# Down projections of a gated block by seven products of quarters instead of eight, with the operand sums formed on the chip

## The chip, the core and the metric

One core of a Trainium2 chip runs the whole program. The metric is the device time of one execution in microseconds (us), the median of several; less is better. The engines named here are PE (TensorE, matrix products), DVE (VectorE), ACT (ScalarE), POOL (GpSimd) and SP (SyncE, which issues most of the transfers). Each runs its own list of instructions in order, and semaphores order them against each other.

## The reference, cut to what matters

The model has two layers on 1024 tokens of width 1024. The part that is changed is the gated block at the end of each layer, with `D_FF` = 2816:

```python
def conv_glu(h, up, conv, down):
    z = dwconv3(h @ up, conv)
    gate, val = jnp.split(z, 2, -1)
    return (jax.nn.gelu(gate, approximate=True) * val) @ down
```

`h @ up` is (1024 x 1024) by (1024 x 5632), and the last product, called down here, is (1024 x 2816) by (2816 x 1024). In layer 0 the result goes on through `x + gt2 * rmsnorm(y, ...)` into the Fourier mixer of layer 1; in layer 1 it gives the output.

## The kernel before

Every large product is made in three passes on numbers split in two: a matrix is rounded to a high part on ACT (`hi`), the rest is subtracted out on DVE or POOL (`lo`), and PE runs hi by hi, hi by lo and lo by hi (`split_products`, L131 to L133). A matmul instruction takes a 128x128 stationary tile and 512 moving columns.

`conv_glu` runs once for each layer. Its **up** part goes over 22 groups `g` of 128 gate and 128 value channels. The first two are plain; the other 20 (`seven`) form the 2x2 product of quarters with seven products, so a group is 7 x 4 x 3 = 84 matmuls. POOL forms the sums of weight quarters and the low parts (L3138, L3151 to L3162), three products ahead of PE (`RING` = 3); DVE adds the seven results up in PSUM (L3236 to L3255), convolves (L3190, L3193) and multiplies by the gelu (L3199, `product`); SP stores each group's activation to `scr_act` in memory. With PSUM banks `ps1` as `in_m1`, `in_m6`, `in_m7` and `ps0` for value and gate, PE waits for DVE before it writes a bank again.

The **down** part takes the token tiles in three runs, 3, 3 and 2 tiles of 128 tokens (`GROUPS`). In each run it goes over the 22 tiles of `down`'s rows (index `q`, 66 steps in all), with 2 x 3 matmuls for each token tile: 8 x 22 x 6 = 1056. Per step ACT makes the high and DVE the low part of a weight tile (128x1024, unless it is among those kept from the first run) and of an activation tile (128x384). POOL does nothing in down. Operand buffers are a ring of three: ACT may write those of step q only when PE has done step q-3 (`after`). The first two steps' operands are made inside the last up group (`split_part(0)`, `split_part(1)`). The rest of a finished run (square, scale by the row norm, add x, and in layer 0 a second norm, a transposition on PE `turn`, and `features`) is spread over the steps of the next run by rules such as `if k == 3 + 5 * i`; it is class `Tail`, and `follows` is true in layer 0 alone.

## Time and profile before

| what | value |
|---|---|
| median of 3 runs | 2735.75 us (2735.1 to 2738.48) |
| profiled execution, its own span | 2735.4 us |
| PE busy in it | 2545.9 us, 93% of the span |
| DVE, ACT, POOL busy | 57%, 42%, 33% |
| layer 0 `conv_glu`: first and last matmul of down | 1597.25 and about 1855 us |
| layer 1 `conv_glu`: first and last matmul of down | 2485.41 and about 2724.6 us |

The time of the profiled execution and its span are the same to 0.3 us. A PE matmul's row shows 0.39 us, but they overlap: the starts of successive ones are what counts. Times in the rows are us from the start of the span.

### The profile page before, as it was taken

The page shows a single profiled execution, that of the slowest core. Times are in us where ns is not written, and L with a number is a line of the kernel's source. Part 1 is how long each engine was busy: PE and PEld are TensorE (multiplying, and loading weights), DVE is VectorE, ACT ScalarE, POOL GpSimd, SP SyncE. Part 2 cuts the span into 40 slices and gives each one's busy share as a digit, 9 for nine tenths or more (in the row PEclk, how much of TensorE's full clock was granted, in tenths as well). Part 3 has the DMA queues.
Part 4 walks back from the last instruction along what each step waited for, and adds up shares of the span by engine and source line. Part 5 has one row for each costly group of instructions (what it writes and reads, how often), then busy time and mean ns, then how long its engine had stood idle before and what let it go on. Part 6 is the DMA issues. An engine that isn't in the chain of part 4 may idle for free. (4 is left out here: it accounts for less than half of the span.)

```text
span 2735.4 us, 51474 instructions
## 1 busy us (share of the span) xinstructions
PE 2545.9 (93%) x21459; PEld 2056.0 (75%) x21459; DVE 1554.7 (57%) x2258; ACT 1158.6 (42%) x1818; POOL 906.6 (33%) x629
## 2 busy tenths in 40 slices
PE   5998989898999989789999999996988999999998
PEld 4776656566888877678888888775767888888887
DVE  7775622464666646655555564456565555556445
ACT  5211252464555533434444444453443434444434
POOL 2301121212222202247877720001324787772000
PEclk7999999998999989999999999998999999999999
DMA  7686534812222123222323265441222232326554
GB/s 241 216 279 218 174 124 168 255 25 75 77 73 73 50 88 132 77 78 85 93 70 93 82 235 187 167 144 72 85 77 80 82 93 70 92 86 237 188 176 146
DMA packets 295914, 346.27 MB, mean 127 GB/s; under 512 B 28383, under 2 KB 224212, under 8 KB 295684
## 3 DMA queue, kind: packets, MB, share of 16 engines
q1 hardware_dynamic: 286044, 336.64, 37.7%
q10 hardware_dynamic: 9640, 6.33, 0.8%
q8 instruction: 172, 2.82, 0.4%
q14 instruction: 58, 0.48, 0.1%
HBM read 271.58 MB, written 71.34 MB: 125 GB/s over the span
## 5 line engine op out<-in xcount | busy, mean ns | idle before, releaser
L3138 POOL TENSOR_TENSOR cg_u_lo<-cg_u_raw,cg_u_hi 128x512 fp32r<-128x512 f32 x210 | 314.5, 1506 | 148.1 <-ACT cg_u_hi L3024 148.1
L131 PE MATMUL cg_ps<-m_hi,cg_u_hi 128*128 128x512 f32 x844 | 331.5, 393 | 26.1 <-DVE cg_u_lo L3213 21.8
L133 PE MATMUL cg_ps<-m_hi,cg_u_lo 128*128 128x512 f32 x844 | 330.8, 392 | 0.0
L132 PE MATMUL cg_ps<-m_lo,cg_u_hi 128*128 128x512 f32 x808 | 316.3, 391 | 0.0
L3024 ACT ACTIVATE cg_u_hi<-cg_u_raw 128x512 fp32r<-128x512 f32 x216 | 132.1, 629 | 381.0 <-PE cg_ps L133 230.6
L131 PEld LDWEIGHTS cg_ps<-m_hi,cg_u_hi 128*128 128x128 f32 x844 | 160.0, 190 | 61.2 <-DVE cg_u_lo L3213 22.6
L133 PE MATMUL cg_ps<-over_y_tx,cg_u_lo 128*128 128x512 f32 x480 | 186.9, 389 | 0.0
L132 PE MATMUL cg_ps<-over_y_tx,cg_u_hi 128*128 128x512 f32 x480 | 186.9, 389 | 0.0
L131 PE MATMUL cg_ps<-over_y_tx,cg_u_hi 128*128 128x512 f32 x480 | 186.9, 389 | 0.0
L133 PEld LDWEIGHTS cg_ps<-m_hi,cg_u_lo 128*128 128x128 f32 x844 | 159.9, 189 | 33.5
L3190 DVE SCALAR_TENSOR_TENSOR cg_z<-cg_ps,top_conv_f,cg_z 128x1023 f32<-128x1023 f32 x88 | 112.9, 1283 | 115.7 <-ACT cg_z L3048 115.7
L132 PEld LDWEIGHTS cg_ps<-m_lo,cg_u_hi 128*128 128x128 f32 x808 | 152.8, 189 | 31.6
L3138 POOL TENSOR_TENSOR cg_u_lo<-cg_u_s,cg_u_hi 128x512 fp32r<-128x512 f32 x80 | 103.6, 1296 | 63.7 <-ACT cg_u_hi L3024 63.7
L3193 DVE SCALAR_TENSOR_TENSOR cg_z<-cg_ps,top_conv_f,cg_z 128x1023 f32<-128x1023 f32 x88 | 112.9, 1283 | 3.1
L131 PE MATMUL za_ps<-h_hi,za_w_hi 128*128 128x512 f32 x256 | 105.8, 413 | 7.4 <-POOL za_w_lo L1039 7.4
L3048 ACT ACTIVATE cg_z<-cg_ps,top_conv_f 128x1024 f32<-128x1024 f32 x88 | 98.2, 1116 | 21.0 <-DVE cg_ps L3250 11.6
L132 PEld LDWEIGHTS cg_ps<-over_y_tx,cg_u_hi 128*128 128x128 f32 x480 | 90.1, 188 | 18.7
L133 PEld LDWEIGHTS cg_ps<-over_y_tx,cg_u_lo 128*128 128x128 f32 x480 | 90.1, 188 | 18.7
L131 PEld LDWEIGHTS cg_ps<-over_y_tx,cg_u_hi 128*128 128x128 f32 x480 | 90.1, 188 | 18.7
L131 PE MATMUL cg_ps<-over_f_d_hi,cg_a_hi 128*128 128x512 f32 x248 | 97.0, 391 | 6.4 <-DVE cg_a_lo L3209 6.4
L132 PE MATMUL za_ps<-h_lo,za_w_hi 128*128 128x512 f32 x256 | 102.8, 402 | 0.0
L133 PE MATMUL za_ps<-h_hi,za_w_lo 128*128 128x512 f32 x256 | 102.4, 400 | 0.0
(497 smaller groups left out, 6216.2 us busy)
## 6 DMA issues: line engine op xcount, KB each, us to landing
cg_u_raw<-in_ffn_up SPq DMA_DIRECT2D x88, 512.0 KB, 5.1
cg_u_raw<-in_ffn_down SPq DMA_DIRECT2D x64, 512.0 KB, 4.8
qkv_mw<-in_ada_w SPq DMA_DIRECT2D x12, 2048.0 KB
over_f_d_raw<-in_ffn_down SPq DMA_DIRECT2D x48, 512.0 KB, 5.0
scr_act<-cg_z SPq DMA_DIRECT2D x44, 512.0 KB, 2.7
qkv_mw<-in_ada_w SPq DMA_DIRECT2D x8, 1024.0 KB, 11.7
next_w<-in_mix_in SPq DMA_DIRECT2D x16, 512.0 KB, 6.0
za_out<-in_ada_w SPq DMA_DIRECT2D x8, 1024.0 KB
```

Source lines behind the costliest of these rows:

```text
L131: nc.tensor.matmul(out, a_hi, b_hi, start=first, stop=False)
L132: nc.tensor.matmul(out, a_hi, b_lo, start=False, stop=False)
L133: return nc.tensor.matmul(out, a_lo, b_hi, start=False, stop=last)
L3024: A(u_hi[:, n % RING], source(g, i), ACT.Copy).then_inc(uhi_done, 1)
L3048: A(z[:, x, :], both(g, x), ACT.Copy, scale=conv_cols[:, 1, g + x * FT:g + x * FT + 1]).then_inc(mid_done, 1)
L3138: G.tensor_tensor(u_lo[:, n % RING], source(g, i), u_hi[:, n % RING].bitcast(F32), ALU.subtract).then_inc(ulo_done, 1)
L3190: V.scalar_tensor_tensor(z[:, x, 1:S], both(g, x)[:, 0:S - 1], conv_cols[:, 0, c:c + 1], z[:, x, 1:S], ALU.mult, ALU.add).then_inc(left_do ...
L3193: V.scalar_tensor_tensor(z[:, x, 0:S - 1], both(g, x)[:, 1:S], conv_cols[:, 2, c:c + 1], z[:, x, 0:S - 1], ALU.mult, ALU.add).then_inc(con ...
```

## The change

The down product is now a 2x2 product of quarters made with seven products instead of eight, with the same algebra as in up. A (activations) is cut by tokens and by channels, B (down weights) by channels and by output columns; `KD` = 11 tiles of 128 channels are half of the 22, and `HT` = 4 token tiles half of the 8. A step is one (product, k) pair with a 128x512 tile of A and one of B and 4 x 3 = 12 matmuls. There are 77 operand steps (`SPLITS`); the last product (`A22T4`, steps from 66) is run as three passes of 11, over 2, 1 and 1 token tiles, on the same operands. That is 7 x 11 x 4 x 3 = 924 matmuls.

The sums of activations (S1 to S4) are formed on DVE in up, from group 12 on, and once more behind group 21: `activation_sums(g-1)` follows `product(g-1)`. Its partner, the activation of 11 groups earlier, is read back by SP (`load_partner`), and the four sums are stored (`store_sums`, 4 transfers of 256 KB) and read again in down. The sums of weights (T1 to T4) are formed on POOL and (T4) on DVE in down. Weights come from memory once. From step 22 to 65 POOL makes the low parts of B, otherwise DVE does. Results that serve two quarters are copied out by ACT (`keep`) or added by DVE and POOL. Three tail operations move from DVE and ACT to POOL (`add_x`, `scale_x` for token tiles 0 to 3).

```diff
-GROUPS = ((0, 1, 2), (3, 4, 5), (6, 7))
...
+KD = FT // 2
+HT = TT // 2
+A11B11, A12B21, S1T1, S4B22, S2T2, S3T3, A22T4 = range(7)
+STEPS = [(p, k, 0, HT) for p in range(6) for k in range(KD)] + [(A22T4, k, i, n) for i, n in ((0, 2), (2, 1), (3, 1)) for k in range(KD)]
+SPLITS = 7 * KD
+LAST = A22T4 * KD
+TAIL_AT = (59, 61, 63, 65)
+
...
+        def raw_b(n):
+            return (of_b11, of_b21, of_b11, of_b22, of_b22, of_b12, of_b21)[n // KD](n % KD)
...
+            def load_partner(g):
+                if g > KD:
+                    sp.wait_ge(asum_stored, 64 * (g - KD))
+                if g == NG - 1:
+                    sp.wait_ge(umm_done, ITEMS)
+                sp.wait_ge(act_stored, 16 * (g - KD + 1))
+                sp.dma_start(flat(sums_of(g)[:, 0:2, :]), act_d[g - KD]).then_inc(partner_loaded, 16)
+
+            def store_sums(g):
+                sp.wait_ge(asum_done, 4 * (g - KD + 1))
+                for i, at in enumerate((2, 0, 1, 3)):
+                    sp.dma_start(sum_d[i, g - KD], sums_of(g)[:, at, :]).then_inc(asum_stored, 16)
...
+            for n in range(4):
+                load_a(n)
             store_act(NG - 2)
+            store_sums(NG - 2)
             sp.wait_ge(ulo_done, ITEMS)
...
+            load_partner(NG - 1)
+            for k in range(5, KD):
+                sp.dma_start(of_b11(k), down_v[k, 0]).then_inc(b11_loaded[k], 16)
...
+            def split_down_a(n):
+                hi, _ = split_a_to(n)
+                if n >= LAST:
+                    act.wait_ge(a22_loaded[n - LAST], 16)
+                    low_b(act, n)
+                else:
+                    if n == 0:
+                        act.wait_ge(asum_stored, 64 * (SETS - 1))
+                    elif n == 2:
+                        act.wait_ge(umm_done, ITEMS)
+                    elif n >= 3:
+                        after(act, n - 3)
+                    act.wait_ge(a_loaded[n % RAWS], 16 * (n // RAWS + 1))
+                A(hi, raw_a(n), ACT.Copy).then_inc(ahi_done, 1)
...
+            def keep(n):
+
+                for i in range(HT):
+                    if n == A11B11:
+                        product_done(act, n, i)
+                        A(y[:, HT + i, 0:HALF], ps[1][:, i, :], ACT.Copy).then_inc(p1_kept, 1)
...
-                    if g == NG - 1:
-                        split_part(0)
-                        split_part(1)
                     for i in range(2, 5):
                         ahead(n + i + RING)
+                    if g == NG - 1:
+                        for j in range(2):
+                            split_down_a(j)
+                            split_down_b(j)
                     middle(g, VAL)
                     for i in range(5, 7):
                         ahead(n + i + RING)
                     middle(g, GATE)
-            split_part(2)
+            split_down_a(2)
+            split_down_b(2)
             gelu(NG - 1)
...
+            for k in range(KD):
...
+                low_b(pool, k)
+                weight_sum(of_b11(k), of_b12(k), of_b11(k), t1_sum)
+            for k in range(KD):
+                pool.wait_ge(b22_loaded[k], 16)
+                pool.wait_ge(t1_sum, k + 1)
+                weight_sum(of_b12(k), of_b22(k), of_b12(k), t3_sum)
+            for n in range(2 * KD, LAST):
+                p, k = divmod(n, KD)
+                low_weights(n)
+                if p == S4B22:
+                    pool.wait_ge(t3_sum, k + 1)
+                    pool.wait_ge(blo_pool, n - 2 * KD + 1)
+                    weight_sum(of_b22(k), of_b22(k), of_b11(k), t2_sum)
+                if n == S3T3 * KD + 2:
+                    for i in range(HT):
+                        pool.wait_ge(u2_sum, i + 1)
+                        pool.wait_ge(p5_kept, i + 1)
+                        G.tensor_tensor(y[:, HT + i, HALF:D], y[:, HT + i, HALF:D], y[:, HT + i, 0:HALF], ALU.add).then_inc(u4_sum, 1)
+                for t, at in enumerate(TAIL_AT):
+                    if n == at + 1:
+                        tail.add_x(pool, G, t, y[:, t, :])
+                    if n == at + 4 and follows:
+                        scale_x(t)
...
+                z0, z1 = z[:, GATE, 0:HALF], z[:, GATE, HALF:S]
+                p0, p1, s1, s4 = (sums_of(g)[:, i, :] for i in range(4))
+                m = 4 * (g - KD)
+                dve.wait_ge(partner_loaded, 16 * (g - KD + 1))
+                dve.wait_ge(glu_done, g + 1)
+                V.tensor_tensor(s1, p1, z1, ALU.add).then_inc(asum_done, 1)
+                dve.wait_ge(asum_done, m + 1)
+                V.tensor_tensor(p1, p0, p1, ALU.subtract).then_inc(asum_done, 1)
+                dve.wait_ge(asum_done, m + 2)
+                V.tensor_tensor(p0, s1, p0, ALU.subtract).then_inc(asum_done, 1)
+                dve.wait_ge(asum_done, m + 3)
+                V.tensor_tensor(s4, z0, p0, ALU.subtract).then_inc(asum_done, 1)
...
+                    if g > KD:
+                        activation_sums(g - 1)
...
+                    if g == NG - 1:
+                        for j in range(2):
+                            low_down_a(j)
+                            low_down_b(j)
                     convolve(g, GATE)
-            split_part(2)
+            low_down_a(2)
+            low_down_b(2)
             product(NG - 1)
+            activation_sums(NG - 1)
+            for n in range(3, SPLITS):
+                low_down_a(n)
+                if n < 2 * KD:
+                    low_down_b(n)
+                if S2T2 * KD <= n < S2T2 * KD + KD:
+                    last_weight_sum(n - S2T2 * KD)
+                if 46 <= n < 46 + KD:
+                    low_down_b(LAST + n - 46)
...
+                if n == S3T3 * KD + 1:
+                    for i in range(HT):
+                        product_done(dve, S2T2, i)
+                        dve.wait_ge(p1_kept, i + 1)
+                        V.tensor_tensor(y[:, HT + i, 0:HALF], ps[1][:, i, :], y[:, HT + i, 0:HALF], ALU.add).then_inc(u2_sum, 1)
...
+                if n == LAST + 1:
+                    for i in range(HT):
+                        product_done(dve, S3T3, i)
+                        dve.wait_ge(u4_sum, i + 1)
+                        V.tensor_tensor(y[:, HT + i, HALF:D], ps[1][:, i, :], y[:, HT + i, HALF:D], ALU.add).then_inc(y22_done, 1)
+                for t, at in enumerate(TAIL_AT):
+                    if n == at + 1:
+                        residual(t)
...
+            def down(n):
+                p, k, first_tile, count = STEPS[n]
+                at = n if n < SPLITS else LAST + k
+                more = p in (A12B21, S4B22, A22T4)
+                side_of = ps[0] if p in (S1T1, S4B22) else ps[1]
+                (a_hi, a_lo), (b_hi, b_lo) = split_a_to(at), split_b_to(at)
+                pe.wait_ge(alo_done, at + 1)
+                low_b(pe, at)
+                for i in range(first_tile, first_tile + count):
+                    tile = slice(i * P, (i + 1) * P)
+                    if k == 0:
+                        if p == A11B11:
                             pe.wait_ge(u3_done, NG - PLAIN)
+                        elif p == A12B21:
+                            pe.wait_ge(p1_kept, i + 1)
+                        elif p == S1T1:
+                            pe.wait_ge(conv_done, 2 * NG)
+                        elif p == S4B22:
+                            pe.wait_ge(p5_kept, i + 1)
+                        elif p == S2T2:
+                            pe.wait_ge(y11_done, i + 1)
+                        elif p == S3T3:
+                            pe.wait_ge(u2_sum, i + 1)
+                        else:
+                            pe.wait_ge(y22_done, i + 1)
```

Two places in the order of instructions. First **DVE in the last up group (g = 21) of layer 0** and behind it. `cg0_z` is the activation, `cg0_u2`, `cg0_u3`, `cg0_m1` hold partial results; a `_lo` tile is a low part. Before:

```order
L3199 TENSOR_TENSOR cg0_z<-cg0_z 128x1024
L3207 TENSOR_TENSOR over_f_d_lo<-over_f_d_raw,over_f_d_hi 128x1024
L3209 TENSOR_TENSOR cg0_a_lo<-cg0_a_raw,cg0_a_hi 128x384
L3207 TENSOR_TENSOR over_f_d_lo<-over_f_d_raw,over_f_d_hi 128x1024
L3209 TENSOR_TENSOR cg0_a_lo<-cg0_a_raw,cg0_a_hi 128x384
L3245 TENSOR_TENSOR cg0_u2<-cg0_ps0,cg0_u2 128x512
L3248 TENSOR_TENSOR cg0_ps0<-cg0_ps0,cg0_u3 128x512
L3250 TENSOR_TENSOR cg0_ps0<-cg0_ps0,cg0_u3 128x512
L3190 SCALAR_TENSOR_TENSOR cg0_z<-cg0_ps0,top_conv_f,cg0_z 128x1023
L3193 SCALAR_TENSOR_TENSOR cg0_z<-cg0_ps0,top_conv_f,cg0_z 128x1023
L3253 TENSOR_TENSOR cg0_ps0<-cg0_ps0,cg0_m1 128x512
L3255 TENSOR_TENSOR cg0_ps0<-cg0_ps0,cg0_u2 128x512
```

Of the change, from the last sum of group 20 to the operands of steps 0 and 1:

```order
L3398 TENSOR_TENSOR cg0_over_ring_sums<-cg0_z,cg0_over_ring_sums 128x512
L3455 TENSOR_TENSOR cg0_u2<-cg0_ps0,cg0_u2 128x512
L3458 TENSOR_TENSOR cg0_ps0<-cg0_ps0,cg0_u3 128x512
L3460 TENSOR_TENSOR cg0_ps0<-cg0_ps0,cg0_u3 128x512
L3374 SCALAR_TENSOR_TENSOR cg0_z<-cg0_ps0,top_conv_f,cg0_z 128x1023
L3377 SCALAR_TENSOR_TENSOR cg0_z<-cg0_ps0,top_conv_f,cg0_z 128x1023
L3463 TENSOR_TENSOR cg0_ps0<-cg0_ps0,cg0_m1 128x512
L3465 TENSOR_TENSOR cg0_ps0<-cg0_ps0,cg0_u2 128x512
L3403 TENSOR_TENSOR cg0_a_lo<-cg0_u_raw,cg0_a_hi 128x512
L3408 TENSOR_TENSOR cg0_b_lo<-raw_over_f_b,cg0_b_hi 128x512
L3403 TENSOR_TENSOR cg0_a_lo<-cg0_u_raw,cg0_a_hi 128x512
L3408 TENSOR_TENSOR cg0_b_lo<-raw_over_f_b,cg0_b_hi 128x512
```

The four operations that make operands for steps 0 and 1 stood ahead of the two convolutions and wait for ACT alone; now they stand behind `L3465`, the last addition of the group. A little further on DVE comes to the operands of steps 2 and 3, with the product and the sums of group 21 between them (`y0_x` holds that last set):

```order
L3403 TENSOR_TENSOR cg0_u_lo<-cg0_u_raw,cg0_u_hi 128x512
L3408 TENSOR_TENSOR cg0_u_lo<-raw_over_f_b,cg0_u_hi 128x512
L3383 TENSOR_TENSOR cg0_z<-cg0_z 128x1024
L3392 TENSOR_TENSOR y0_x<-y0_x,cg0_z 128x512
L3394 TENSOR_TENSOR y0_x<-y0_x 128x512
L3396 TENSOR_TENSOR y0_x<-y0_x 128x512
L3398 TENSOR_TENSOR y0_x<-cg0_z,y0_x 128x512
L3403 TENSOR_TENSOR cg0_a_lo<-cg0_u_raw,cg0_a_hi 128x512
L3408 TENSOR_TENSOR cg0_b_lo<-raw_over_f_b,cg0_b_hi 128x512
```

Step 2's operands stand ahead of `L3383`, step 3's behind the four sums. Now **ACT at the same place**, before:

```order
L3052 ACTIVATE cg0_z<-cg0_z 128x1024
L3062 ACTIVATE over_f_d_hi<-over_f_d_raw 128x1024
L3065 ACTIVATE cg0_a_hi<-cg0_a_raw 128x384
L3062 ACTIVATE over_f_d_hi<-over_f_d_raw 128x1024
L3065 ACTIVATE cg0_a_hi<-cg0_a_raw 128x384
L3024 ACTIVATE cg0_u_hi<-cg0_u_raw 128x512
L3024 ACTIVATE cg0_u_hi<-cg0_u_s 128x512
L3048 ACTIVATE cg0_z<-cg0_ps0,top_conv_f 128x1024 x2
```

and of the change:

```order
L3135 ACTIVATE cg0_z<-cg0_z 128x1024
L3107 ACTIVATE cg0_u_hi<-cg0_u_raw 128x512
L3107 ACTIVATE cg0_u_hi<-cg0_u_s 128x512
L3150 ACTIVATE cg0_a_hi<-cg0_u_raw 128x512
L3173 ACTIVATE cg0_b_hi<-raw_over_f_b 128x512
L3150 ACTIVATE cg0_a_hi<-cg0_u_raw 128x512
L3173 ACTIVATE cg0_b_hi<-raw_over_f_b 128x512
L3131 ACTIVATE cg0_z<-cg0_ps0,top_conv_f 128x1024 x2
```

The two middle copies (`cg0_z<-cg0_ps0`) followed the up splits; now four splits of down stand ahead of them, the first of which waits until the sums of group 20 are stored. Last, **POOL in steps 56 to 63** of down, where before it had no instruction (`L3315` is a low part of B, `L3338` the additions to `y`, `L2341` add_x, `L3278` scale_x):

```order
L3315 TENSOR_TENSOR cg_u_lo<-raw_over_f_b,cg_u_hi 128x512
L3315 TENSOR_TENSOR cg_b_lo<-raw_over_f_b,cg_b_hi 128x512
L3338 TENSOR_TENSOR y_y<-y_y 128x512 x4
L3315 TENSOR_TENSOR cg_b_lo<-raw_over_f_b,cg_b_hi 128x512
L3315 TENSOR_TENSOR cg_u_lo<-raw_over_f_b,cg_u_hi 128x512
L3315 TENSOR_TENSOR cg_b_lo<-raw_over_f_b,cg_b_hi 128x512
L2341 TENSOR_TENSOR y_x<-y_x,y_y 128x1024
L3315 TENSOR_TENSOR cg_b_lo<-raw_over_f_b,cg_b_hi 128x512
L3315 TENSOR_TENSOR cg_u_lo<-raw_over_f_b,cg_u_hi 128x512
L2341 TENSOR_TENSOR y_x<-y_x,y_y 128x1024
```

## Rows read from the trace of the kernel before

**Rows 1.** The page, part 1: busy us, share of the span, instructions.

```profile
PE 2545.9 (93%) x21459; PEld 2056.0 (75%) x21459; DVE 1554.7 (57%) x2258; ACT 1158.6 (42%) x1818; POOL 906.6 (33%) x629
```

**Rows 2.** Windows: one up group, down's middle, a tail; busy us, clock, DMA, GB/s.

```profile
1457.00:1476.04 19.04, 19.04 (x86) 15.77 (x85) 11.05 (x13) 7.98 (x11) 15.02 (x12) 1.00 0.27 83
...
1597.00:1620.00 23.00, 22.31 (x99) 18.14 (x98) 15.67 (x18) 10.37 (x14) 0.00 (x0) 1.00 0.81 299
...
2600.00:2724.60 124.60, 124.60 (x551) 103.22 (x550) 61.25 (x79) 51.30 (x80) 0.00 (x0) 1.00 0.50 164
```

**Rows 3.** Timeline, PE: first matmuls of down in both layers, and one turn.

```profile
1597.25 0.39 PE L131 MATMUL cg_ps<-over_f_d_hi,cg_a_hi 128*128 128x512 f32 x1
...
1825.50 1.03 PE L2352 MATMUL cg_ps<-top_ident,y_y 128*128 128x128 f32 x8
...
2485.41 0.39 PE L131 MATMUL cg_ps<-over_f_d_hi,cg_a_hi 128*128 128x512 f32 x1
```

**Rows 4.** Timeline, ACT: squares of the last token tile of each layer.

```profile
1855.22 1.02 ACT L2261 ACTIVATE over_h_rows<-cg_ps 128x1024 f32<-128x1024 f32 x1
...
2725.94 1.02 ACT L2261 ACTIVATE over_h_rows<-cg_ps 128x1024 f32<-128x1024 f32 x1
```

**Rows 5.** Timeline, DVE, one steady group of up; in brackets idle before.

```profile
1464.17 0.70 DVE L3255 TENSOR_TENSOR cg_ps<-cg_ps,cg_u 128x512 f32<-128x512 f32 x1 [0.34 <-PE cg_ps L133]
...
1467.37 1.28 DVE L3193 SCALAR_TENSOR_TENSOR cg_z<-cg_ps,top_conv_f,cg_z 128x1023 f32<-128x1023 f32 x1
...
1472.94 1.22 DVE L3199 TENSOR_TENSOR cg_z<-cg_z 128x1024 f32<-128x1024 f32 x1
```

**Rows 6.** Timeline, POOL, in the same group.

```profile
1458.30 1.29 POOL L3151 TENSOR_TENSOR cg_u_s<-cg_u_raw 128x512 f32<-128x512 f32 x1 [0.17 <-POOL cg_u_lo L3138]
...
1462.35 1.30 POOL L3157 TENSOR_TENSOR cg_u_raw<-cg_u_s,cg_u_raw 128x512 f32<-128x512 f32 x1
1464.53 2.55 POOL L3138 TENSOR_TENSOR cg_u_lo<-cg_u_raw,cg_u_hi 128x512 fp32r<-128x512 f32 x2 [0.89 <-ACT cg_u_hi L3024]
...
1473.10 2.20 POOL L3138 TENSOR_TENSOR cg_u_lo<-cg_u_raw,cg_u_hi 128x512 fp32r<-128x512 f32 x1 [0.16 <-ACT cg_u_hi L3024]
```

**Rows 7.** Timeline, DVE and POOL in layer 0's last up group.

```profile
1589.45 1.65 DVE L3209 TENSOR_TENSOR cg_a_lo<-cg_a_raw,cg_a_hi 128x384 fp32r<-128x384 f32 x1
...
1593.26 0.55 DVE L3209 TENSOR_TENSOR cg_a_lo<-cg_a_raw,cg_a_hi 128x384 fp32r<-128x384 f32 x1
...
1588.82 1.87 POOL L3138 TENSOR_TENSOR cg_u_lo<-cg_u_raw,cg_u_hi 128x512 fp32r<-128x512 f32 x1 [1.64 <-ACT cg_u_hi L3024]
1590.64 1.61 POOL L3138 TENSOR_TENSOR cg_u_lo<-cg_u_s,cg_u_hi 128x512 fp32r<-128x512 f32 x1
```

**Rows 8.** One line's ns min/median/max; then groups: total us, mean ns | idle.

```profile
L3213 DVE TENSOR_TENSOR cg_u_lo<-cg_u_raw,cg_u_hi x6: 683/692/693, 1169.7 to 2060.8; 128x512 fp32r<-128x512 f32 x6
...
L2309 DVE SCALAR_TENSOR_TENSOR y_y<-y_y,cg_t_rstd,over_h_rows 128x1024 f32<-128x1024 f32 x12 | 15.4, 1286 | 0.4
...
L3024 ACT ACTIVATE cg_u_hi<-cg_u_s 128x512 fp32r<-128x512 f32 x80 | 50.4, 629 | 80.1 <-PE cg_ps L133 78.9 <-issue 1.2
...
L3545 POOL TENSOR_TENSOR m_lo<-fft_over_f_f,m_hi 128x1024 fp32r<-128x1024 f32 x8 | 18.9, 2363 | 45.9 <-ACT m_hi L3510 45.9
```

**Rows 9.** Timeline, PE, after 10.26 us and after 2.93 us of idleness.

```profile
1170.42 0.80 PE L131 MATMUL cg_ps<-m_hi,cg_u_hi 128*128 128x512 f32 x1 [10.26 <-DVE cg_u_lo L3213]
...
1175.63 0.40 PE L131 MATMUL cg_ps<-m_hi,cg_u_hi 128*128 128x512 f32 x1
...
1812.88 0.47 PE L131 MATMUL cg_ps<-m_hi,cg_u_hi 128*128 128x512 f32 x1 [2.93 <-DVE cg_u_lo L3209]
...
1817.30 0.39 PE L131 MATMUL cg_ps<-over_f_d_hi,cg_a_hi 128*128 128x512 f32 x1
```

**Rows 10.** Issue of a store on SP (ns min/median/max); transfers, KB, us to landing.

```profile
L2958 SPq DMA_DIRECT2D scr_act<-cg_z x44: 320/339/339, 1208.8 to 2495.4; - x44
...
scr_act<-cg_z SPq DMA_DIRECT2D x44, 512.0 KB, 2.7
...
cg_u_raw<-in_ffn_down SPq DMA_DIRECT2D x64, 512.0 KB, 4.8
```

476 lines of the change are left out of this document (294 added, 182 removed).

## The prediction

> **What bounds the kernel now.** The page's first lines say that PE is the engine that counts: 93% of the span, with DVE at 57%, ACT at 42% and POOL at 33% [rows 1]. The windows by stage say how it differs inside `conv_glu` [rows 2]: in a steady up group PE is busy for all of 19.04 us at full clock, beside DVE 11.05 and POOL 15.02; in down PE is full again while POOL has nothing. Down of layer 1 runs from 2485.41 [rows 3] to the last tile's square at 2725.94 [rows 4], the matmuls ending about 2724.7: 1056 matmuls in 239.4 us, 0.2267 us each (a group of 84 is 19.04). Down of layer 0 runs from 1597.25 to about 1855.1, 257.9 us: 239.4 of matmuls, six turns inside at up to 1.0 us [rows 3], and 12.5 us of waits, one of 2.93 [rows 9]. So fewer matmuls shorten the span only while ACT, DVE and POOL deliver operands within the new, shorter steps.
>
> Two things of this trace decide how well they can. First, **DVE and POOL block each other** when DVE reads two SBUF operands [rows 7]: a 384-wide subtraction takes 0.55 us alone, but 1.65 when POOL has got in first; POOL's, begun at 1588.82, ends at 1590.69, the DVE one 0.41 later, and POOL's next, begun at 1590.64, shows 1.61 instead of 1.29: it ends at 1592.25, 1.15 after DVE's 1591.10. They alternate. For 512 columns DVE takes 0.69 alone [rows 8] and, once it has waited, 0.14 less, 0.55; POOL takes 1.29 alone [rows 6] and 1.15 once it has waited. Additions with one operand in PSUM show no such wait (0.70 with POOL busy) [rows 5, 6]. Second, **a pause of PE costs more than itself** [rows 9]: after 10.26 us idle the next twelve matmuls take 5.21 us (1170.42 to 1175.63) where 2.72 is usual, so 2.5 more at the 1.2 GHz level; after 2.93 idle, 4.42, so 1.7 more.
>
> **What is won.** 132 matmuls a layer less, 264 x 0.2267 = 59.9 us. Layer 0's 12.5 us of waits belong to rules that are gone; I count them as won and cost the new waits below. At the end one token tile is left instead of two: in layer 1 what follows the last matmul is one addition (0.70), a square (1.5), reciprocal and scale (1.4) and add (1.2) beside two scales and adds in series, 1.5 us less; in layer 0 I estimate 2.5 less. Together 76.4 us.
>
> **Start of down (S).** Times from the last up group's start, taken from the steady group, which begins at 1464.0 (PE ended just ahead of the addition at 1464.17) [rows 5]. The product of group 20, at 8.9 there (1472.94), comes at about 10.6 to 11.8, since the sums of the group before push DVE (below). Four sums, chained, with POOL's last low part between: 15.8. SP issues four stores at 0.34 each, the last lands 2.7 after its issue [rows 10]: 19.9. Only then does ACT split steps 0 and 1 (4 x 0.56 back to back, 0.63 alone [rows 8]): 22.2, then the value copy 1.12: 23.4. DVE: two convolutions 2.6, two additions 1.3, 27.4; a and b of step 0 1.3: 28.7. PE finished up at 19.1: **9.6 us idle**. In before these splits stood ahead and PE went on without a gap [rows 3]. Then steps 0 to 2 run to 37.7 (0.8 lost on step 2, whose low parts stand behind a convolution). Step 3's stand behind product 21 (ends 36.1), a 512 KB store, the partner's load (lands near 41; 2.7 to 4.8 after its issue [rows 10]) and four sums (44.1): ready at 45.4. PE waits **7.8** more. S = 18.2 a layer, 36.4; bounds 13 and 22 (sums without blocking and landing in 2.7; 4.8 twice). The two pauses a layer bring 4 x 2.5 = 10 us of low clock.
>
> **Up groups with sums (U),** ten a layer. POOL's run from `L3151` to the next group's second low part ends at 1465.8, PE needs it at 1466.7: 0.9 us to spare [rows 6]. The sums fall on that run; each waits one POOL operation and pushes one: the four take 5.9 us, POOL is late by two or three times 0.55. PE loses about 0.6 a group, 12 us in all. Low end 0. High end: if DVE becomes the bound with 11.05 of work, 2.4 waiting for the two middle copies [rows 5] and 4 x (0.69 + 1.29) for the sums, 21.4 us a group, 2.3 more than 19.04: 46.
>
> **Steps 22 to 54 (CD).** A step is 12 x 0.2267 = 2.72 us. In S1T1 the port has DVE 0.69 and POOL 1.29, which fits. In S4B22 POOL has two: 0.55 + 1.15 + 1.29 + 0.1 for its own semaphore = 3.1. With three buffers POOL begins 2.65 us early, which is used up in seven of eleven steps; 1.5 us lost. In S2T2 DVE has three and POOL one: 0.69 + 1.15 + 0.55 + 0.61 = 3.0, and nothing is to spare: 3.1 lost. 4.6 a layer, and 0.7 at step 22, whose POOL operation stands behind the last T3 sum: 10.6 in all. Bounds: 0, were the lead never used up, and 20, were each operation at 0.69 + 1.29. Of this port the Trainium skill says the same as the rows (SBUF — State Buffer, Who interferes with whom: a DVE instruction with two SBUF inputs and a POOL one that reads SBUF exclude each other for the whole instruction). It goes further than they do for `scale_y`, which reads two SBUF operands: the row has 1.286 us with POOL idle [rows 8], by which each costs nothing new; by the rule each of the four beside POOL work could wait one operation, some 5 us more over both layers. No row of before shows it.
>
> **Steps 55 to 76 (E).** Step 55 needs `u2_sum`, which DVE makes behind two low parts for steps 56 and 76; without the backlog it would be ready 0.8 us late, with it 4.9. At step 57 POOL makes four additions (5.2 us); the lead covers that. At 60, 62, 64 it makes add_x, 2.36 each [rows 8], between low parts that PE waits for, and add_x waits for a square on ACT and scale_y on DVE: by step, 1.5 at step 61 and 0.2 at 63. Layer 1: 4.9 + 1.7 = 6.6. In layer 0 ACT's `square_x` waits for POOL's add_x ahead of the next split, and scale_x comes on top: worked through, 1.5, 1.8, 1.2 and 1.4 at steps 61, 62, 63, 65, and step 66 waits for additions behind the fourth residual, `features` and step 67's split (up to 4.8): 15.6. Sum 22.2; bounds 8 and 34. The long pause at 55 costs 1.7 of clock in each layer, 3.4; the last two turns inside layer 0 another 2.5.
>
> **The sum.** Lost: 36.4 + 10 + 12 + 10.6 + 22.2 + 3.4 + 2.5 = 97.1. Won: 76.4. The span 2735.4 becomes 2756; the median of the runs shown, 2735.75, stands 0.35 above the span, so **2756 us**. What hides nothing: loads. A step reads 512 KB in 2.72 us, 193 GB/s, where the trace moves 299 with PE busy [rows 2]; if they did bound, each step would be longer by what the rows don't show, and I give that no more than 2 in 100.
>
> **The rivals.** (1) Faster: the lead of three steps takes up the port's waits and DVE comes in time to step 55. Then U and CD are near 0, E is near 8, and 36.4 + 10 + 8 + 3 = 57 is lost: 2716. For it: PE loses nothing in before's last up group although DVE and POOL alternate there [rows 7]; against: there no further group depends on POOL. It decides when everything except S and its clock stays under 30 us. A half-way case, S shorter by 5 us a layer and the others halved, gives about 2722. Chance of faster 0.33. (2) DVE becomes the bound of the ten groups, U 46: 2790. For it, 4 sums on an engine that already waits twice a group; against, POOL is paced by PE and not always ready. 0.12. (3) Gains and losses cancel within 0.2%: 0.1. My forecast, losses ahead of gains by 6 to 45 us: 0.45.
>
> **How the numbers follow.** 0.2% is 5.5 us and about what can be told apart. The low end 2714 is rival 1; the high end 2784 takes U half-way to rival 2 with E at its high end. Forecast's own range 2742 to 2776. Slower 0.57, same 0.1, faster 0.33.
>
> **What the profile after would show.** PE 264 matmuls fewer. S: in both layers a pause of 8 to 11 us before the first matmul of down and one of 6 to 9 three steps later, each with a stretch of low clock behind it; ACT's first split of down waiting for a store. U: groups 12 to 21 some 0.6 us longer than 19.04, with POOL subtractions of 1.8 us and DVE sums of 1.7. CD: steps of 3.0 to 3.1 us in S4B22 and S2T2. E: a pause at step 55, and PE waiting for POOL from step 61 on. Groups at 19.04 and down steps at 2.72 outside S would make me wrong on the fast side; groups above 21 on the slow side.

## The result and the profile after

The changed kernel took 2772.99 us in the median of 4 runs (2769.25 to 2781.95) beside 2737.11 us of the kernel before on the same chip (2735.1 to 2743.28): a ratio of 1.0129, with a 95% interval of 1.0107 to 1.0151. It is slower, by about 36 us. The profiled execution took 2769.25 us, with a span of 2767.3, which is 31.8 more than the span of before. (In all runs behind the prediction the time stands about 2 us above the span, and not 0.3.)

The page's first part, which answers to [rows 1]: PE has its 264 matmuls fewer and is busy for 33 us less in a span that is longer. DVE has 180 us more, POOL 295 more.

```profile
PE 2512.8 (91%) x21195; PEld 2009.8 (73%) x21195; DVE 1735.2 (63%) x2368; ACT 1155.7 (42%) x1890; POOL 1201.4 (43%) x803
```

The windows, columns as in [rows 2]: one up group of layer 0 that makes sums, and the start of down.

```profile
1463.69:1484.53 20.84, 19.65 (x85) 15.58 (x84) 18.05 (x17) 7.65 (x12) 16.40 (x11) 1.00 0.47 152
1617.20:1640.20 23.00, 16.55 (x56) 13.08 (x57) 16.54 (x19) 6.59 (x11) 9.79 (x6) 0.77 0.67 239
```

The group lasts 20.84 us and not 19.04; DVE is busy in it for 18.05 (11.05 in before). At the start of down PE works 16.55 us of 23, at a granted clock of 0.77, where it worked 22.31 at full clock in before.

The timeline of that group on DVE (L3374 and L3377 convolve, L3383 is the product, L3392 to L3398 are the four sums, L3460 is the addition that ACT's copy of the value bank waits for):

```profile
1463.69 1.28 DVE L3374 SCALAR_TENSOR_TENSOR cg_z<-cg_ps,top_conv_f,cg_z 128x1023 f32<-128x1023 f32 x1 [1.19 <-ACT cg_z L3131]
...
1468.68 1.29 DVE L3374 SCALAR_TENSOR_TENSOR cg_z<-cg_ps,top_conv_f,cg_z 128x1023 f32<-128x1023 f32 x1 [1.19 <-ACT cg_z L3131]
...
1472.60 2.02 DVE L3383 TENSOR_TENSOR cg_z<-cg_z 128x1024 f32<-128x1024 f32 x1
1474.71 1.60 DVE L3392 TENSOR_TENSOR cg_over_ring_sums<-cg_over_ring_sums,cg_z 128x512 f32<-128x512 f32 x1
1476.35 1.67 DVE L3394 TENSOR_TENSOR cg_over_ring_sums<-cg_over_ring_sums 128x512 f32<-128x512 f32 x1
1478.04 1.67 DVE L3396 TENSOR_TENSOR cg_over_ring_sums<-cg_over_ring_sums 128x512 f32<-128x512 f32 x1
1479.74 1.67 DVE L3398 TENSOR_TENSOR cg_over_ring_sums<-cg_z,cg_over_ring_sums 128x512 f32<-128x512 f32 x1
...
1482.65 0.69 DVE L3460 TENSOR_TENSOR cg_ps<-cg_ps,cg_u 128x512 f32<-128x512 f32 x1
1484.53 1.28 DVE L3374 SCALAR_TENSOR_TENSOR cg_z<-cg_ps,top_conv_f,cg_z 128x1023 f32<-128x1023 f32 x1 [1.19 <-ACT cg_z L3131]
```

DVE idles in two places only, 1.19 us each, for ACT's copies. The product takes 2.02 where it took 1.22 [rows 5]. On ACT, POOL and PE the lateness is handed on:

```profile
1483.37 1.12 ACT L3131 ACTIVATE cg_z<-cg_ps,top_conv_f 128x1024 f32<-128x1024 f32 x1 [5.81 <-DVE cg_ps L3460]
1484.39 1.14 ACT L3107 ACTIVATE cg_u_hi<-cg_u_raw 128x512 fp32r<-128x512 f32 x2
...
1485.15 2.53 POOL L3274 TENSOR_TENSOR cg_u_lo<-cg_u_raw,cg_u_hi 128x512 fp32r<-128x512 f32 x2 [1.16 <-ACT cg_u_hi L3107]
...
1486.48 0.50 PE L131 MATMUL cg_ps<-over_y_tx,cg_u_hi 128*128 128x512 f32 x1 [0.85 <-POOL cg_u_lo L3274]
```

PE's wait names POOL; POOL waits for the split at 1484.39 on ACT, which stands behind the copy at 1483.37, and that one has waited 5.81 us for DVE. The last engine named is not the one that is slow.

The timeline of the start of down: PE in layer 0, then in layer 1 (these answer to [rows 3]), and what it waited for, on ACT (L3150 is the split of the first step) and on DVE.

```profile
1617.23 0.76 PE L3617 MATMUL cg_ps<-cg_b_hi,cg_a_hi 128*128 128x512 f32 x1 [9.93 <-DVE cg_a_lo L3403]
1633.72 0.76 PE L3617 MATMUL cg_ps<-cg_b_hi,cg_a_hi 128*128 128x512 f32 x1 [6.42 <-DVE cg_b_lo L3408]
...
2521.77 0.77 PE L3617 MATMUL cg_ps<-cg_b_hi,cg_a_hi 128*128 128x512 f32 x1 [9.96 <-DVE cg_a_lo L3403]
2538.78 0.76 PE L3617 MATMUL cg_ps<-cg_b_hi,cg_a_hi 128*128 128x512 f32 x1 [6.95 <-DVE cg_b_lo L3408]
...
1608.91 0.63 ACT L3150 ACTIVATE cg_a_hi<-cg_u_raw 128x512 fp32r<-128x512 f32 x1 [9.05 <-DMA scr_asum<-cg_over_ring_sums]
...
1629.50 0.69 DVE L3392 TENSOR_TENSOR y_x<-y_x,cg_z 128x512 f32<-128x512 f32 x1 [5.15 <-DMA y_x<-scr_act]
```

Two pauses per layer, each with the store or load named that the prediction named; behind each, as in [rows 9], a step at the low clock (4.5 to 4.7 us and not 2.72). And one that it did not name, behind step 33 in both layers:

```profile
1719.63 2.02 DVE L2296 TENSOR_TENSOR over_h_rows<-over_h_rows 128x1024 f32<-128x1024 f32 x1 [6.15 <-DMA over_h_rows<-in_norm_g]
...
1723.44 0.80 PE L3617 MATMUL cg_ps<-cg_b_hi,cg_a_hi 128*128 128x512 f32 x1 [3.20 <-DVE cg_a_lo L3403]
...
2628.51 0.79 PE L3617 MATMUL cg_ps<-cg_b_hi,cg_a_hi 128*128 128x512 f32 x1 [3.12 <-DVE cg_a_lo L3403]
```

`row_gain` (L2296, which multiplies the gate row by the norm row for the tails) stands on DVE behind step 33's low part, but SP asks for its rows only at step 41 of its own loop, after it has waited for that low part: DVE cannot have them sooner than a transfer after it.

**The ledger**, from the starts of PE's first and last matmul of up and of down in both traces, after less before: ahead of layer 0's up, −4.9 us (stages that the change does not touch); up, 441.4 against 426.6 us and 441.5 against 426.0, +30.3; from the last up matmul to the last one of down, 259.1 against 257.8 in layer 0 and 246.0 against 240.3 in layer 1, +7.0, although 59.9 us of matmuls are gone (before's last matmul starts at 2725.5, 0.9 later than the table ahead of the prediction has it); the rest −0.4. Sum +32. In down the change gives back all that it wins and 7 us more; the up groups make most of the loss.

### The profile page after: what moved, and what is told of

It reads as the page before. It is cut to its first block and busy times, and to the rows that moved or that the text cites. A ratio compares the mean times of both kernels' runs of the same rounds, so it can differ in the third digit from the quotient of the medians.

```text
span 2767.3 us, 51616 instructions
## 1 busy us (share of the span) xinstructions
PE 2512.8 (91%) x21195; PEld 2009.8 (73%) x21195; DVE 1735.2 (63%) x2368; ACT 1155.7 (42%) x1890; POOL 1201.4 (43%) x803
## 5 line engine op out<-in xcount | busy, mean ns | idle before, releaser
L131 PE MATMUL cg_ps<-m_hi,cg_u_hi 128*128 128x512 f32 x768 | 303.0, 394 | 26.7 <-DVE cg_u_lo L3427 21.4
L133 PE MATMUL cg_ps<-m_hi,cg_u_lo 128*128 128x512 f32 x768 | 300.4, 391 | 0.0
L3374 DVE SCALAR_TENSOR_TENSOR cg_z<-cg_ps,top_conv_f,cg_z 128x1023 f32<-128x1023 f32 x88 | 112.9, 1283 | 121.7 <-ACT cg_z L3131 121.7
L3617 PE MATMUL cg_ps<-cg_b_hi,cg_a_hi 128*128 128x512 f32 x352 | 144.0, 409 | 49.5 <-DVE cg_a_lo L3403 26.2
L3618 PE MATMUL cg_ps<-cg_b_lo,cg_a_hi 128*128 128x512 f32 x352 | 141.8, 403 | 0.0
L3619 PE MATMUL cg_ps<-cg_b_hi,cg_a_lo 128*128 128x512 f32 x352 | 141.4, 402 | 0.0
L3403 DVE TENSOR_TENSOR cg_a_lo<-cg_u_raw,cg_a_hi 128x512 fp32r<-128x512 f32 x88 | 81.9, 931 | 89.5 <-ACT cg_a_hi L3150 89.5
L131 PEld LDWEIGHTS cg_ps<-over_y_tx,cg_u_hi 128*128 128x128 f32 x480 | 90.0, 188 | 41.2 <-POOL cg_u_lo L3274 21.7
L3617 PEld LDWEIGHTS cg_ps<-cg_b_hi,cg_a_hi 128*128 128x128 f32 x352 | 69.1, 196 | 69.8 <-DVE cg_a_lo L3403 42.6
L3150 ACT ACTIVATE cg_a_hi<-cg_u_raw 128x512 fp32r<-128x512 f32 x88 | 55.5, 631 | 151.6 <-PE cg_ps L3619 133.5
L1039 POOL TENSOR_TENSOR za_w_lo<-next_w,za_w_hi 128x1024 fp32r<-128x1024 f32 x16 | 39.0, 2438 | 178.6 <-ACT za_w_hi L897 178.6
```

Source lines behind the costliest of these rows:

```text
L131: nc.tensor.matmul(out, a_hi, b_hi, start=first, stop=False)
L133: return nc.tensor.matmul(out, a_lo, b_hi, start=False, stop=last)
L3150: A(hi, raw_a(n), ACT.Copy).then_inc(ahi_done, 1)
L3374: V.scalar_tensor_tensor(z[:, x, 1:S], both(g, x)[:, 0:S - 1], conv_cols[:, 0, c:c + 1], z[:, x, 1:S], ALU.mult, ALU.add).then_inc(left_do ...
L3403: V.tensor_tensor(lo, raw_a(n), hi.bitcast(F32), ALU.subtract).then_inc(alo_done, 1)
L3617: nc.tensor.matmul(out, a_hi[:, tile], b_hi, start=start, stop=False, skip_group_check=more)
```

## The experiments

In what follows the steps of a run are told by the starts of PE's matmuls: an undisturbed step takes 2.72 us, a product 29.92.

**late_last_sums**: the second pause alone. On DVE:

```diff
             product(NG - 1)
-            activation_sums(NG - 1)
             for n in range(3, SPLITS):
                 low_down_a(n)
                 if n < 2 * KD:
                     low_down_b(n)
+                if n == 5:
+                    activation_sums(NG - 1)
```

> One change to the changed kernel: VectorE makes the four sums of the last feature tile not right behind product 21, ahead of the low parts of step 3, but behind those of step 5. Theory: the second pause (6.42 and 6.95 us before step 3, and two steps of 4.5 to 4.7 us at the low clock) is there only because step 3's low parts stand behind a store, a load and four sums, so it goes: step 3 starts with no wait over 1.5 us in both layers, no pause of that size comes back at steps 6 to 12, and the time falls by 14 to 18 us, to 2755 to 2759. The first pause (9.9 us) stays. Rival: product 21, the conversion and its own backlog hold VectorE in any case, so a pause of 3 to 5 us remains at steps 3 to 6 and the gain is under 7 us.

Ratio 1.0071 (1.0046 to 1.0097), 2757.51 us. Step 3 follows without a wait in both layers, and the first eleven steps take 33.4 and 33.5 us where they took 40.3 and 40.5. A wait of 1.5 us has appeared at step 6, behind the sums, and layer 0 loses 1.3 and 1.7 again in the fourth and sixth product, so that in the profiled run layer 0's down is 3.5 us shorter and layer 1's 6.8. By the ratios the gain is 16 us, as expected; the two profiled executions differ by 9 only. The theory holds; a part is given back.

**rows_early**: the pause behind step 33. On SP:

```diff
-                if n == 41:
+                if n == 28:
                     tail.load_rows(sp)
```

> One change to the changed kernel: the sync queue issues the loads of the gate and norm rows (and the columns) at step 28 of its own loop and not at step 41. Theory: VectorE's row_gain at step 33 waits 6.15 us for loads that the queue issues only when the low part of step 33 is done; that is the pause of 3.2 and 3.1 us at steps 33 and 34 and the slow steps there (6.1, 4.3). With the loads early, steps 33 to 35 take 2.7 to 2.9 us each in both layers and the time falls by 9 to 12 us, to 2761 to 2764. Rival: the pause comes from VectorE and GpSimd on their shared port in the products S4B22 and S2T2 (steps of 3.0 us, as predicted): then steps 33 and 34 gain less than 2 us together and the whole under 4 us.

Ratio 1.0173 (1.0144 to 1.0202), 2784.74 us: slower than the change itself. Both theories had a piece of it. Steps 33 to 35 take 2.72 each, and then come 2.86, six of 3.12 to 3.15 and one of 3.35: with the pause gone, S4B22 runs at the port's pace, 33.2 us in both layers, as the prediction had it. In the kernel as changed POOL ran no faster: its low parts of S4B22 behind the pause start 3.03 us apart (1729.16 to 1750.37, seven steps), and the lead that the pause had given it kept PE's steps at 2.72. And the loads went out among those of quarter B22. SP, layer 0:

```profile
1685.99 4.67 SPq L2239 DMA_DIRECT2D cg_t_scale<-scr_mod  x1
1690.71 0.58 SPq L3038 DMA_DIRECT2D cg_u_raw<-scr_asum  x1
1691.34 0.43 SPq L3078 DMA_DIRECT2D raw_over_h_b<-in_ffn_down  x1
...
1694.63 1.26 POOL L3310 TENSOR_TENSOR raw_over_f_b<-raw_over_h_b,raw_over_f_b 128x512 f32<-128x512 f32 x1 [7.32 <-DMA raw_over_h_b<-in_ffn_down]
...
1697.21 0.76 PE L3617 MATMUL cg_ps<-cg_b_hi,cg_a_hi 128*128 128x512 f32 x1 [5.62 <-issue]
```

The column load holds SP for 4.67 us, the last weights of B22 are asked for behind it, POOL's last T3 sum waits 7.32 for them, and the low part of step 22, which stands behind that sum, ends at 1697.1: PE starts at 1697.21, after 5.62 us. (The row's "issue" means only that its semaphore shows no later event.) The column load is not all of it: layer 1 loads no columns, and there the last T3 sum still waits 4.03 us for its weights and PE 2.43 in front of step 22, behind the two row loads.

**no_up_sums** and **no_up_transfers**: is it DVE's work or the traffic that lengthens the up groups? The first lets DVE signal without adding; the second takes the operands from DVE's own product and leaves the transfers out.

```diff
# no_up_sums, in activation_sums(g)
+                if g < NG - 1:
+                    dve.sem_inc(asum_done, 4)
+                    return
# no_up_transfers, in activation_sums(g) and on SP
-                V.tensor_tensor(s1, p1, z1, ALU.add).then_inc(asum_done, 1)
+                V.tensor_tensor(s1, z0, z1, ALU.add).then_inc(asum_done, 1)
-                if g > KD:
-                    store_sums(g - 1)
-                if g >= KD:
-                    load_partner(g)
```

> Leaves out VectorE's four activation sums in up groups 12 to 21 of each layer; the partner tiles are still loaded and four halves of them are stored in place of the sums, so the transfers and the semaphores are as in the changed kernel. Theory (VectorE is the bound of these groups: four sums of 1.65 us beside 11 of its own work and two waits of 1.19): groups 12 to 20 fall from 20.84 to 19.0 to 19.1 us, 16 to 18 us per layer, time 2735 to 2742. Rival (the transfers, 1.5 MB more per group, slow the loads of weights): the groups stay above 20.3. The pauses at the start of down stay, shorter by at most 4 us in each layer.

> Leaves out the loads of the partner tiles and the stores of the sums; VectorE makes four additions of the same shape from the halves of its own product (two SBUF operands each, at the same places), and down loads products where it loaded sums. Theory (engines, not transfers): groups 12 to 20 stay at 20.7 to 20.9 us. Rival (transfers): they fall to 19.0 to 19.3. In either case the first pause of down is shorter by the store, some 3 us to about 7, and the second by the load of the partner, to 0 to 3 us; time about 2750 to 2756 by the first theory.

One run each: 2723.21 and 2757.87 us. Windows of one group, no_up_sums ahead, no_up_transfers behind:

```profile
1462.50:1481.54 19.04, 19.04 (x86) 15.77 (x85) 11.05 (x12) 7.97 (x11) 15.02 (x12) 1.00 0.53 166
...
1464.00:1484.84 20.84, 19.70 (x86) 15.60 (x86) 18.12 (x17) 7.64 (x11) 16.41 (x12) 1.00 0.24 77
```

Without the sums, and with twice the traffic of the other, all groups take 19.04; with the sums and without the traffic, 20.84, as in the changed kernel. It is the sums. Without them the one run was at 0.995 of the median of before on its chip (2736.34), below the 2735 to 2742 that I expected. Not all of that is the up groups: PE's first pause in down is 5.06 and 5.52 us there and not 9.9, so that the run doesn't show what the rest of the change is worth. In no_up_transfers, where no store is waited for, the first pause is still 5.55 us in both layers: more than half of it needs no store.

**step0_early**: the first pause alone. The four halves of step 0 are moved out from under the sums' buffer, so that only step 1 waits for the stores.

```diff
-                    if n == 0:
+                    if n == 1:
                         act.wait_ge(asum_stored, 64 * (SETS - 1))
...
                     if g == NG - 1:
-                        for j in range(2):
-                            split_down_a(j)
-                            split_down_b(j)
+                        split_down_a(0)
+                        split_down_b(0)
                     middle(g, VAL)
```

> One change to the changed kernel: the four halves of step 0 lie outside the buffer of the activation sums, so that ScalarE splits step 0 ahead of the conversion of the value bank without a wait, VectorE makes its low parts behind the addition of item 5, and only step 1 waits for the stores of the sums (split behind the value bank, low parts ahead of the gate convolution). Theory: the first pause (9.9 us) goes to under 1 us, with small pauses of 1 to 2 us at steps 1 and 2, but product 21, the store, the partner's load and the four sums end hardly sooner, so that the second pause grows from 6.4 to 7.0 to 10 to 13 us: down starts about 10 us sooner in each layer and step 3 only 3 to 4 us sooner. Time 2762 to 2768. Rival (the two pauses are independent): the second stays at 6.4 to 7 and the time falls by 17 to 22 us, to about 2753.

Ratio 1.0088 (1.0072 to 1.0103), 2760.38 us. The first pause is gone (a wait of 0.41 us), 2.05 and 0.79 come back at steps 1 and 2 of layer 0, and the second grows little: from step 2's start to step 3's it takes 9.9 and 11.6 us where it took 9.3 and 9.8. So step 3 starts 19.5 and 21.6 us behind the last up matmul and not 26.8 and 27.4, and with the longer low clock 6.9 and 4.6 us are kept of a pause of 9.9. That lies between the theory, which gave step 3 only 3 to 4 us, and the rival: the pauses are coupled, but by less than I had said.

**sums_in_gaps**: the same work in another order, to tell a busy DVE from a pushed POOL. The third and fourth sum stand where DVE waits for ACT's copies.

```diff
                     V.tensor_tensor(bank(g, VAL, 0), bank(g, VAL, 0), u3[:, :], ALU.add).then_inc(c21_done, 1)
+                    if spread:
+                        sum_4(g - 1)
...
                     V.tensor_tensor(bank(g, GATE, 1), bank(g, GATE, 1), u2[:, :], ALU.add).then_inc(c12_done, 1)
+                    if spread:
+                        sum_3(g - 1)
```

> One change to the changed kernel: in up groups 12 to 20 VectorE makes two of the four sums behind the product as before, one while ScalarE copies the value bank and one while ScalarE copies the gate bank (a fifth half in the buffer of the sums makes the order free). Same work, same transfers, as many conflicts on the port. Theory (VectorE is the bound: busy for all of 20.84 us but the two waits of 1.19): these groups fall to 19.0 to 19.5 us, the time by 24 to 33 us, to 2740 to 2749. Rival (as put on record in the prediction: the sums push GpSimd's run off, each by half a microsecond, and VectorE has room): the order changes nothing, groups 20.5 to 20.9.

Ratio 1.0113 (1.009 to 1.0137), 2769.11 us: an inconclusive time and a telling trace. Layer 0's groups 13 to 20 take 19.06, 19.29, 19.52, 23.07, 19.20, 19.46, 23.09, 19.40; layer 1's 19.07 to 20.42, with one of 23.48. The order does matter, against the rival; but the stores end later, the next partner tile waits for them, and DVE for it:

```profile
1481.31 1.35 DVE L3404 TENSOR_TENSOR cg_over_ring_sums<-cg_over_ring_sums,cg_z 128x512 f32<-128x512 f32 x1 [4.42 <-DMA cg_over_ring_sums<-scr_act]
```

**tail_later**: PE's waits for POOL from step 60 on. `TAIL_AT` becomes (63, 65, 67, 69).

> One change to the changed kernel: the tails of the first four token tiles begin at steps 63, 65, 67 and 69 and not at 59, 61, 63 and 65, so that most of GpSimd's add_x and scale_x fall behind its last low part (step 65). Theory: PE waits at steps 60 to 65 for low parts that stand behind add_x on GpSimd. In layer 1 these six steps fall from 20.3 us in sum to 17 to 18, in layer 0 from 28.8 (two turns in them) to 19 to 22, of which 3 to 5 us come back behind step 66. Time 2759 to 2765. Rival: the work is only shifted and the steps behind 66, which take 1.36 us each, wait as long: gain under 3 us.

Ratio 1.0161 (1.0147 to 1.0175), 2779.67 us: a miss. The product S3T3 does fall, from 42.5 to 35.3 us in layer 0 and from 35.6 to 31.4 in layer 1, but steps 66 to 76 rise from 20.0 to 32.8 and from 15.0 to 24.4. A step there is 1.36 us, half of one before, and has its own low part; the same tail work finds less room than it left. In layer 1 PE waits there for DVE, and DVE waits 4.46 for a split on ACT.

**low_on_dve**: the port in S4B22 and the late rows together. Rows and columns are asked for at SP's step 31, and DVE makes the low parts of S4B22.

```diff
         def on_pool(n):
-            return 2 * KD <= n < LAST
+            return 2 * KD <= n < LAST and n // KD != S4B22
...
-                if n == 41:
+                if n == 31:
                     tail.load_rows(sp)
```

> Two changes to the changed kernel: the row and column loads at step 31 of the sync queue (behind the last quarter-B22 load), and the low parts of the weights of product S4B22 on VectorE (0.69 us) and not on GpSimd (1.29). Theory: the pause of steps 33 and 34 is row_gain's wait for rows asked for too late, and once it is gone the port binds (rows_early: steps of 3.13 with two GpSimd operations each); with 1.38 us of VectorE and 1.29 of GpSimd a step fits 2.72. Product S4B22 takes 30 to 31 us in both layers where it took 34.9 and 36.1, S2T2 stays near 33.5; time 2760 to 2765. Rival: steps of 3.1 us stay in S4B22 although GpSimd has one operation only; then VectorE's own waits for ScalarE bind, and the time stays above 2768.

Ratio 1.0102 (1.0083 to 1.012), 2764.59 us. The interval of the time overlaps the changed kernel's; the product decides. S4B22 takes 29.92 us in both layers, eleven steps of 2.72, where rows_early had 33.2 and the changed kernel 34.9 and 36.1. POOL has one operation a step, and DVE's take what they take alone, or little more:

```profile
1736.61 1.30 POOL L3312 TENSOR_TENSOR raw_over_h_b<-raw_over_h_b 128x512 f32<-128x512 f32 x1 [1.29 <-DVE cg_b_lo L3411]
...
1737.74 0.72 DVE L3406 TENSOR_TENSOR cg_a_lo<-cg_u_raw,cg_a_hi 128x512 fp32r<-128x512 f32 x1 [1.27 <-ACT cg_a_hi L3152]
1738.38 0.68 DVE L3411 TENSOR_TENSOR cg_b_lo<-raw_over_h_b,cg_b_hi 128x512 fp32r<-128x512 f32 x1
```

**two_pairs**: sums_in_gaps with two pairs of halves for the partner tiles, so that the load need not wait for the last stores.

> Like sums_in_gaps (two sums behind the product, one in each wait for ScalarE's copies), but the partner tiles alternate between two pairs of halves, so that the next one is loaded before the sums of the last are stored (seven halves of buffer and not four). In sums_in_gaps VectorE stood 2.9 and 4.4 us for a partner's load that had to wait for the later stores, and two or three groups took 23 us. Theory: that wait was what was left, and with it gone groups 12 to 20 take 19.0 to 19.5 us in both layers; time 2740 to 2748. Rival: the groups stay uneven, 19.3 to 20.4 with some at 23, since the stores of the sums now stand on the queue ahead of the loads of weights; then the time stays above 2760.

Ratio 1.0101 (1.0076 to 1.0126), 2766.55 us, and the groups as uneven as before (19.04 to 20.33, one of 23.23, one of 21.51 in layer 0): the rival's side, so far. SP shows why the buffer changed nothing: the partner's load was still issued behind the stores and the weights.

```profile
1496.27 1.79 SPq L3027 DMA_DIRECT2D scr_asum<-cg_over_ring_sums  x4
1498.11 1.49 SPq L3010 DMA_DIRECT2D cg_u_raw<-in_ffn_up  x2
1499.69 1.24 SPq L3022 DMA_DIRECT2D cg_over_ring_sums<-scr_act  x1
...
1506.57 1.44 DVE L3420 TENSOR_TENSOR cg_over_ring_sums<-cg_over_ring_sums,cg_z 128x512 f32<-128x512 f32 x1 [3.57 <-DMA cg_over_ring_sums<-scr_act]
```

**combined**, **combined_tail** and **combined_ahead** put the parts together, each with the one before in it. The core of the first is what stands above; the second adds, and the third:

```diff
# combined_tail
-            return 2 * KD <= n < LAST and n // KD != S4B22
+            return n // KD in (S1T1, S2T2)
# ... in residual(t); GpSimd's add_x and scale_x of tiles 0 to 3 go
-                if t >= HT:
-                    dve.wait_ge(tail.x_done, t)
-                    tail.add_x(dve, V, t, y[:, t, :])
+                tail.add_x(dve, V, t, y[:, t, :])
# ... on ScalarE
+                    if n == at + 4 and follows:
+                        tail.scale_x(act, t)
# combined_ahead, on SP
+                if g >= KD:
+                    load_partner(g)
                 if g > KD:
                     store_sums(g - 1)
                 if g + 2 < NG:
                     load_up(g + 2)
-                if g >= KD:
-                    load_partner(g)
```

> All at once: two_pairs; step 0 split without waiting for the sums' stores, steps 1 to 3 ahead of the gate convolution and of the last product; the last four sums behind step 8; the loads of quarter B11 ahead of the last store; the row and column loads at step 31; the low parts of S4B22 on VectorE; the additions that step 55 waits for ahead of step 56's low parts. Theory: the terms found one by one (up groups 15 to 18 us a layer, both pauses at the start of down 17 to 20, steps 33 to 43 6.6, step 54 1 to 2) add up once they are removed together, since none of them can then be given back to the next: 36 to 42 us less per layer, time 2690 to 2705, and faster than the kernel before. Rival: each pause was cover for the next, as in step0_early, so that half comes back: 2725 to 2745.

> combined, and in steps 55 to 76 GpSimd has nothing but four additions: the low parts of S3T3 and add_x of the first four tiles are on VectorE, scale_x of these on ScalarE. Theory: steps 60 to 65 (28.8 us in layer 0, 20.3 in layer 1 in the changed kernel) waited for low parts behind add_x on the slower engine and on the port; VectorE has 0.69 + 0.69 + half of 1.28 + half of 1.22 a step, 2.6 us of 2.72, so layer 1 loses at most 1 us there and layer 0 at most 4 beside its turns; 6 to 12 us less than combined. Rival: VectorE, at 2.6 of 2.72, falls behind and the steps from 61 on wait for it as long as they did for GpSimd: no less than combined.

> combined_tail, and on the sync queue the load of a group's partner tile is issued ahead of the stores of the last sums and of the two loads of weights, where it stood behind them (a semaphore of its own for each of the two pairs). In two_pairs the load was issued at 1499.69, behind four stores and two weight loads, and VectorE stood 3.57 us for it before the first sum. Theory: with the wait gone the groups with sums are bound by PE again: groups 12 to 20 at 19.0 to 19.3 us in both layers and none at 23, 7 to 10 us less per layer than combined_tail, time 2690 to 2698. Rival: the unevenness comes from weights that arrive late, since their loads stand behind the stores of the sums; then the groups stay at 19.4 to 20.4 and the time above 2704.

The ratios are 0.9948 (0.9933 to 0.9964), 0.9899 (0.9879 to 0.992) and 0.9822 (0.9795 to 0.985), the medians 2723.33, 2710.16 and 2686.41 us. The first has both pauses gone (the first eleven steps 34.3 us, behind a wait of 0.39) and S4B22 at 29.92, but its groups are as uneven as in two_pairs, so it misses its 2705 and ends just below the rival's 2725. The second gains 13 us more, with S3T3 at 32.1 us in layer 1, nothing lost behind step 57; in layer 0 it takes 40.3, more than the 4 us over matmuls and turns that I gave it. One step there is 8.1 us: behind a turn PE waits for the additions that free the banks of S3T3, and these stand on DVE behind the tail's work, so in this place the rival had it right:

```profile
1808.48 0.77 PE L3659 MATMUL cg_ps<-split_over_h_t 128*128 128x512 f32 x1 [4.25 <-DVE y_y L3545]
```

The third has all groups with sums at 19.04 to 19.08 us in both layers, which makes up 11.5 us shorter in each, and a time of 2686, below the 2690 to 2698 that I expected. It is 1.8% faster than the kernel before. Its window of one group:

```profile
1464.00:1483.06 19.06, 19.06 (x85) 15.71 (x85) 16.64 (x18) 8.00 (x11) 16.11 (x11) 1.00 0.53 166
```

The four sums are all there, and PE is full beside them. So the unevenness was the partner's load on the queue, and what the three experiments on the groups took to be one cause was two, in a row: DVE's full period, and behind it the place of one load on SP. Layer 1's down takes 217.5 us, 209.5 of it matmuls (924 x 0.2267).

## Why the prediction was right in sign and low in size

The forecast was 2756 and slower; it came to 2773, inside the range. By its own steps:

- **S**, 36.4 us: 9.93 and 9.96 us for the first pause where it had 9.6, 6.42 and 6.95 for the second where it had 7.8, and nothing at step 2 where it had 0.8: 33.3. Cause and place are shown, by late_last_sums and step0_early. What the sum didn't have is that the two are not independent: each removed alone is worth 7 us or less a layer in the profiled executions.
- **Low clock**, 10: steps 0 and 3 took 4.47 and 4.74 us in layer 0, 4.46 and 4.49 in layer 1; over 2.72 that is 7.3 in sum.
- **U**, 12: the term that was mis-sized. It is 30.3 us, 1.8 in each of groups 14 to 20 and less in 13 and 21; group 12 lost nothing. The step that failed is "The sums fall on that run; each waits one POOL operation and pushes one ... PE loses about 0.6 a group". It followed POOL's lateness and did not add up DVE's own period, though all the figures stood in it: 11.05 of work, 2.4 of waits for the copies, 5.9 for the sums make 19.35 already, over 19.04, and with the product blocked too (0.8 more) and the four sums at the 6.6 that they took it is 20.85. (That it meets the measured 20.84 so closely is luck: the group's row has 18.05 of work, 2.4 of waits and 0.4 in gaps too short to be listed.) The rival "DVE becomes the bound" had this mechanism, at 21.4, and was given 0.12. no_up_sums and no_up_transfers show that it is the sums; combined_ahead, with the same sums, shows that it is DVE's period: two of them fill the waits, and the blocking is less by 1.4 us a group (16.64 us busy and not 18.05). How much each of these two gave was not parted.
- **CD**, 10.6: right only in total, by luck. But for step 35 of layer 1 (3.08, behind the pause) PE has no step of 3.0 to 3.1 us in these products; 4.9 and 6.2 us went in product S4B22, at the pause of steps 33 to 35 that the prediction had no term for. It counted the work of DVE and POOL there and not where SP asks for the rows. The mechanism that it did name is real, and larger than said: rows_early brought it out as 3.3 us a layer in S4B22 against 1.5. In S2T2 it is on DVE, whose three operations a step take 2.90 us, one of them 1.78; PE pays for the backlog at steps 52 and 53, 3.45 and 2.90 us, and at step 55:

```profile
1767.61 1.78 DVE L3412 TENSOR_TENSOR raw_over_h_b<-raw_over_h_b 128x512 f32<-128x512 f32 x1
...
1770.52 1.77 DVE L3412 TENSOR_TENSOR raw_over_h_b<-raw_over_h_b 128x512 f32<-128x512 f32 x1
...
1777.55 0.50 PE L3617 MATMUL cg_ps<-cg_u_hi 128*128 128x512 f32 x1 [0.57 <-DVE cg_u_lo L3403]
...
1785.86 0.47 PE L3617 MATMUL cg_ps<-cg_b_hi,cg_a_hi 128*128 128x512 f32 x1 [2.35 <-DVE y_y L3491]
```

- **E** with its clock, 25.6: what steps 44 to 54, 55 to 65 and 66 to 76 take over their matmuls comes to 3.7, 10.5 and 2.9 us in layer 0 beside the turns and to 3.5 and 5.7 in layer 1, 26.3 in all. The wait at step 55 is 2.35 and not 4.9; add_x on POOL took 2.76 where it had 2.36, and pushed low parts that PE waited for up to 2.16, as said. The last two turns inside layer 0 cost 3.0 where it had 2.5.
- **Won**, 76.4: the 59.9 of matmuls and layer 0's 12.5 came; the 4 us of tails did not: 9.9 us follow the start of layer 1's last matmul, as in before. One tile is left and not two, but it has an addition more on DVE ahead of its square, and its chain starts no sooner. On ACT the last square answers to [rows 4], 1.2 us behind the start of the last matmul (2757.37), where it was 0.4:

```profile
2758.57 1.06 ACT L2261 ACTIVATE cg_z<-y_y 128x1024 f32<-128x1024 f32 x1 [4.17 <-DVE y_y L3514]
```

With these sizes in place of its own the sum comes to 2774, and the stages ahead of up, which ran 4.9 us shorter for no reason in the change, take it to within 2 us of the span. So the account closes, and U is most of the miss.

Of the port: at `scale_y`, for which the prediction left two readings, the summary of the 16 executions in down has a longest of 2142 ns (seven took 2.05 or more, each begun while POOL was at work):

```profile
L2309 DVE SCALAR_TENSOR_TENSOR y_y<-y_y,cg_t_rstd,over_h_rows x16: 1283/1285/2142, 1796.7 to 2760.3; 128x1024 f32<-128x1024 f32 x16
```

That agrees with the rule of the Trainium skill (SBUF — State Buffer, Who interferes with whom) that a DVE instruction with two SBUF operands and a POOL instruction that reads SBUF exclude each other, which [rows 8] could not show. Additions with an operand in PSUM stay at 0.67 to 0.70, beside POOL too, in all runs.

Steps 33 to 35 and 55 differ by 1 to 1.6 us between the layers, and from run to run in kernels that don't touch them. That is the clock. In front of step 55 PE waits 2.35 us in both layers; in layer 0 it then runs at full clock and the step takes 2.81 us, in layer 1 it runs mostly at the lower level and takes 4.42 (windows, columns as in [rows 2]):

```profile
1786.00:1789.00 3.00, 3.00 (x14) 2.48 (x15) 3.00 (x6) 0.13 (x1) 3.00 (x3) 1.00 0.17 66
2692.00:2695.00 3.00, 2.94 (x8) 2.37 (x9) 3.00 (x6) 0.00 (x0) 3.00 (x3) 0.59 0.20 67
```

What stays open is why the same wait lowers the clock once and not the other time, and, in U, how much the filled waits gave and how much the lesser blocking. E was not taken apart: combined_tail moved three kinds of work at once.

## What to carry to other kernels

Before work is put on an engine that "has room", write out that engine's own period: its work, each operation that the shared port will lengthen, and the waits inside the period that it can't fill; room is what is left of that, not the idle share. Pauses in a chain of queues are cover for one another: removed singly they come back in part a few steps on (step0_early, late_last_sums), or make room for the next limit (rows_early, tail_later); removed together, with the sums spread and the tail's work moved, they turned a loss of 1.3% into a gain of 1.8%. For each operation that waits for a transfer, find the line where the transfer is asked for and what stands ahead of it on that queue: here both the pause behind step 33 and, once the sums were spread, the uneven up groups came from such a place.

## What was not expected of the hardware

- Three loads of 1024 single values into columns, one behind the other, took 0.43, 1.01 and 4.67 us to issue on the sync queue in rows_early. The third is slow in the changed kernel as well (3.26 us), where a row load takes 0.43. Everything behind them on the queue is late by that much.
- Two-operand additions in SBUF on DVE took 1.57 to 1.68 us in the mean beside a busy POOL, 0.69 alone; where they stood in the waits for ACT (sums_in_gaps, combined_ahead) they took 0.68 to 1.58, so the place changes the price too.
- A tiny operation with SBUF operands (column_gain, 128x8) took 1.22 us beside POOL, and 0.16 and 0.17 at its two other places in the program.
